# A decoder layer's mixture of experts on one core: chunk of tiles in another order, bias rows and stored residual issued by GpSimd

## The reference, cut to what matters

```python
logits = xt @ w_router + b_router                    # xt: 288 x 1024
top_v, top_i = lax.top_k(logits, 4)
wts = softmax(top_v)
gate_dense = sum(one_hot(top_i, 32) * wts[..., None], axis=1)
out = 0
for e in range(32):                                  # w_up[e]: 1024 x 2048, w_down[e]: 1024 x 1024
    z = xt @ w_up[e] + b_up[e]
    gate = minimum(z[:, :1024], 7.0)
    up = clip(z[:, 1024:], -7.0, 7.0)
    act = (up + 1.0) * gate * sigmoid(1.702 * gate)
    ...                                              # (act @ w_down[e] + b_down[e]), weighted by gate_dense[:, e], is added to out
y = y + g2 * rms_norm(out, norm_ffn_post)            # y: the residual
```

## Time and profile before

| | us |
|---|---|
| median of 3 runs | 1520.52 (1515.4 to 1522.12) |
| the profiled execution's own time | 1513.15 |
| its span, first to last instruction | 1511.3 |
| TensorE busy (matmuls) | 1340.2, 89% of the span |
| TensorE weight loads | 632.4, 42% |
| VectorE, ScalarE, GpSimd busy | 394.7, 254.5, 26.7 |
| moved by DMA | 503.94 MB, mean 333 GB/s |
[...]

### The profile page before, as it was taken

One profiled execution on the slowest core, in us unless ns is written; L12 is line 12 of the kernel. 1 busy time (PEld: TensorE's weight loads), 2 busy tenths in 40 slices (PEclk: granted clock), 3 DMA queues, 4 the chain that ended last, 5 costly groups with the idle time before them and its releaser, 6 DMA issues.

```text
span 1511.3 us, 31712 instructions
## 1 busy us (share of the span) xinstructions
PE 1340.2 (89%) x13949; PEld 632.4 (42%) x13949; DVE 394.7 (26%) x982; ACT 254.5 (17%) x613; POOL 26.7 (2%) x40
## 2 busy tenths in 40 slices
PE   4999997899999897999999789999999669798784
PEld 4554555576765332334333233333343114243231
DVE  5220013378544711112112111221221012021112
ACT  4100006557312200001001000100110001010001
POOL 2000004000000000000000000000000000000000
PEclk9999999999999999999999989999999889999997
DMA  9995746123598799899999996698999999999996
GB/s 282 346 307 217 257 170 196 54 75 139 142 264 333 307 423 426 373 388 393 388 425 427 426 423 290 276 391 355 389 395 424 425 423 428 425 425 425 425 426 235
DMA packets 99297, 503.94 MB, mean 333 GB/s; under 512 B 9473, under 2 KB 39321, under 8 KB 64194
## 3 DMA queue, kind: packets, MB, share of 16 engines
q1 hardware_dynamic: 96258, 485.18, 80.7%
q0 software_dynamic: 2944, 17.32, 3.3%
HBM read 496.33 MB, written 10.31 MB: 335 GB/s over the span
## 4 chain that ended last, share of the span: by engine, by line
PE 65%; DMA 25%; DVE 4%; issue 2%; ACT 1%; POOL 1%; SPq 1%; DVEq 0%; ACTq 0%; POOLq 0%
PE psum L1433 18%; DMA arena<-in_w_down 13%; PE psum L1450 10%; DMA arena<-in_w_up 8%; PE psum L1417 4%; PE psum L819 4%; PE psum L1228 3%; PE psum L1059 3%; PE psum L1060 3%; PE psum L1462 3%; PE psum L1437 2%; PE psum L1325 2%; DMA arena<-in_cache_cmp,arena 2%; PE psum L1468 2%; PE psum L832 1%
## 5 line engine op out<-in xcount | busy, mean ns | idle before, releaser
L1433 PE MATMUL psum<-arena 128*32 128x512 f32 x3328 | 404.5, 621 | 86.0 <-DMA arena<-in_w_up 76.7
L1433 PEld LDWEIGHTS psum<-arena 128*32 128x32 f32 x3328 | 99.5, 112 | 356.3 <-issue 266.0
L1450 PE MATMUL psum<-arena 128*32 128x256 f32 x3328 | 194.1, 383 | 16.3 <-DMA arena<-in_w_down 9.5
L2456 DVE TENSOR_SCALAR arena<-psum 128x256 f32<-128x256 f32 x52 | 22.1, 426 | 662.4 <-PE psum L1433 662.4
L1450 PEld LDWEIGHTS psum<-arena 128*32 128x32 f32 x3328 | 102.4, 110 | 88.2 <-DMA arena<-in_w_down 15.0
L1863 ACT ACTIVATE arena<-arena 128x256 f32<-128x256 f32 x52 | 21.7, 417 | 543.3 <-DVE arena L2456 543.3
L1417 PE MATMUL psum<-arena 128*32 128x256 f32 (+1 forms) x1272 | 94.2, 391 | 3.2 <-DVE arena L2425 3.2
L1228 PE MATMUL psum<-arena 128*128 128x288 f32 x256 | 67.9, 411 | 2.9 <-DMA arena<-in_w_in 2.4
L1417 PEld LDWEIGHTS psum<-arena 128*32 128x32 f32 (+1 forms) x1272 | 30.8, 109 | 83.8 <-issue 78.9
L1462 PE MATMUL psum<-arena 32*128 32x256 f32 x864 | 62.5, 403 | 1.1 <-ACT arena L1872 0.6
L1437 PE MATMUL psum<-arena 32*32 32x512 f32 x416 | 57.8, 627 | 0.0
(11 more groups left out here) (445 smaller groups left out, 1246.3 us busy)
## 6 DMA issues: line engine op xcount, KB each, us to landing
arena<-in_w_up SPq DMA_DIRECT2D x128, 2048.0 KB, 27.5
arena<-in_w_down SPq DMA_DIRECT2D x64, 2048.0 KB, 21.9
arena<-in_w_ada SPq DMA_DIRECT2D x12, 2048.0 KB, 12.4
arena<-in_w_in SPq DMA_DIRECT2D x6, 2048.0 KB, 12.2
arena<-in_w_in SPq DMA_DIRECT2D x16, 512.0 KB, 4.0
arena<-in_state_win SPq DMA_DIRECT2D x4, 1024.0 KB, 10.6
arena<-in_w_out SPq DMA_DIRECT2D x1, 4096.0 KB, 18.4
out<-in_state_win SPq DMA_DIRECT2D x1, 4064.0 KB
```

The costliest lines, as they stand in the source:

```text
L1433: last = mm(banks[0][32 * j:32 * j + SLOT].rearrange("p (h c) -> p h c", h=2), xcT[:, q % 2, q // 2], up_cols[n % R_][:, q % 2, j], start= ...
L1450: last = mm(banks[1][32 * j:32 * j + SLOT, 256:512], aT[:, v, 2 * m + h], down_cols[n % R_][:, h, v, j], start=m + v + h == 0, stop=m + v ...
L2456: V.tensor_scalar(gt, banks[0][:, 0:256], 7.0, None, ALU.min).then_inc(S("gate"), 1)
```

## The change

The ordering within a chunk is changed, and who issues what before the first chunk:
- The b_up matmuls move from after q = 0 to after q = 7, and read row group (r + 2) % 4 for column group r. Directly behind them come the four sample tiles of the dispatch (row group j, column group j) and `add_sample` (row group q, column group (q + 1) % 4). These twelve matmuls use twelve different 32*32 tiles of the array (`small_tiles`). Then come the eight prompt matmuls of the dispatch, `add_prompt`, the transposes of the activations, `chunk_T`, `weights_T`. The last transpose of `weights_T` becomes four 32*32 matmuls with the identity.
- The waits for `oneslot` and `yc` go from behind the up products to behind q = 5. VectorE starts on `up_ps`, signalled by the last b_up matmul.
- To have the sample rows at four partition offsets: ScalarE copies three quarters of h2r's sample rows once, VectorE copies `rowf` and `wts` three times each and completes the one-hot of the first chunk by two operations, all before or at the first chunk.
- GpSimd issues the loads of b_up and b_down, and the two stores of the residual. SyncE's list keeps the pieces; piece 6 waits for `out_ps` alone, piece 8 for the third `h2`, piece 9 for the store. The final sample rows lie rotated by one quarter, with their loads and stores.
- ScalarE takes one square root of a constant into a spare column ahead of the last squares.

```diff
@@ -704,20 +704,11 @@
                     sp.wait_ge(S("out_ps"), 5)
-                    sp.wait_ge(S("h2"), 1)
-                    for r in range(4):
-                        sp.dma_start(bias[32 * r:32 * r + E].rearrange("e (h c) -> e h c", h=2),
-                                     A["b_up"][0].rearrange("e (h j c) -> j e h c", h=2, j=4)[r]).then_inc(S("ld_bias"), 16)
-                    for r in range(4):
-                        sp.dma_start(bdown[32 * r:32 * r + E], A["b_down"][0][:, 256 * r:256 * r + 256]).then_inc(S("ld_bdown"), 16)
                 if n == 8:
-                    sp.wait_ge(S("y1"), 5)
-                    sp.dma_start(xd[0:TP].rearrange("(i p) d -> p i d", p=P), x[:, 0:2]).then_inc(S("st_state"), 16)
-                    sp.dma_start(xd[TP:TP + NS], x[0:NS, 2]).then_inc(S("st_state"), 16)
                     sp.wait_ge(S("h2"), 3)
...
                     sp.wait_ge(S("lg_ps"), 3)
-                    sp.wait_ge(S("st_state"), 64)
+                    sp.wait_ge(S("st_x"), 32)
                 load_piece(n)
@@ -1409,20 +1403,39 @@
 
-            def dispatch(first=False):
-                for n, i in enumerate((0, 2, 1)):
-                    if first and n == 2:
+            def first_dispatch():
+                for n, i in enumerate(ORDER):
+                    if n == 2:
                         pe.wait_ge(S("h2"), 3)
                     for j in range(4):
-                        last = mm(banks[5 if first else 1][32 * j:32 * j + SLOT, 256:512], oneslot[0:ROWS[i], i],
-                                  h2r[0:ROWS[i], i, 256 * j:256 * j + 256],
+                        last = mm(banks[5][32 * j:32 * j + SLOT, 256:512], oneslot[0:ROWS[i], i], h2r[0:ROWS[i], i, 256 * j:256 * j + 256],
                                   start=n == 0, stop=n == 2)
+                last.then_inc(S("xr_ps"), 1)
+
+            def dispatch_prompt():
+                for i in range(2):
+                    for j in range(4):
+                        last = mm(banks[1][32 * j:32 * j + SLOT, 256:512], oneslot[:, i], h2r[:, i, 256 * j:256 * j + 256],
+                                  start=False, stop=i == 1)
                 last.then_inc(S("xr_ps"), 1)
...
                 last.then_inc(S("xcT_ps"), 1)
+
+            def small_tiles(e):
+                if e == 0:
+                    pe.wait_ge(S("ld_bias"), 64)
+                for r in range(4):
+                    at = 32 * ((r + 2) % 4)
+                    last = mm(banks[0][32 * r:32 * r + SLOT, :], ident[at:at + E, at + e:at + e + 1].broadcast_to([E, SLOT]),
+                              bias[at:at + E, :], start=False, stop=True)
+                last.then_inc(S("up_ps"), 1)
+                for j in range(4):
+                    mm(banks[1][32 * j:32 * j + SLOT, 256:512], oneslot[32 * j:32 * j + NS, 2], h2r[32 * j:32 * j + NS, 2, 0:256],
+                       start=True, stop=False)
+                add_sample(owT, yc, SLOT, False, False)
 
@@ -1431,11 +1444,10 @@
                         last = mm(banks[0][32 * j:32 * j + SLOT].rearrange("p (h c) -> p h c", h=2), xcT[:, q % 2, q // 2],
-                                  up_cols[n % R_][:, q % 2, j], start=q == 0, stop=q == 7)
-                    if q == 0:
-                        for r in range(4):
-                            mm(banks[0][32 * r:32 * r + SLOT, :], ident[32 * r:32 * r + E, 32 * r + e:32 * r + e + 1].broadcast_to([E, SLOT]),
-                               bias[32 * r:32 * r + E, :], start=False, stop=False)
+                                  up_cols[n % R_][:, q % 2, j], start=q == 0, stop=False)
+                    if q == 5:
+                        pe.wait_ge(S("oneslot"), c + 2)
+                        pe.wait_ge(S("yc"), c + 1)
                     if q % 2:
@@ -1454,8 +1466,10 @@
                     nc.tensor.transpose(banks[0][:, P * i:P * i + P], ow[:, i].rearrange("p q t -> p (q t)"), ident)
-                nc.tensor.transpose(banks[0][:, TP:TP + NS], ow[0:NS, 2].rearrange("p q t -> p (q t)"), ident[0:NS, 0:NS]
-                                    ).then_inc(S("owT_ps"), 1)
+                for q in range(4):
+                    at = slice(32 * q, 32 * q + NS)
+                    last = mm(banks[0][at, TP:TP + NS], ow[at, 2, q], ident[at, at], start=True, stop=True)
+                last.then_inc(S("owT_ps"), 1)
 
@@ -1465,7 +1479,8 @@
                 for q in range(4):
-                    last = mm(banks[3][32 * q:32 * q + NS, 0:256], shares[32 * q:32 * q + r, TP:TP + NS],
+                    at = 32 * ((q + 1) % 4)
+                    last = mm(banks[3][at:at + NS, 0:256], shares[32 * q:32 * q + r, TP:TP + NS],
                               rows[32 * q:32 * q + r, 0:256], start=start, stop=stop)
@@ -1482,7 +1497,7 @@
             pe.wait_ge(S("oneslot"), 1)
-            dispatch(True)
+            first_dispatch()
             after(pe, "nch")
@@ -1493,7 +1508,7 @@
             add_sample(zeros, zeros, SLOT, True, False)
-            pe.wait_ge(S("ld_bias"), 64)
+            pe.wait_ge(S("h2s"), 3)
 
@@ -1505,18 +1520,16 @@
                     up_products(c, e)
-                    pe.wait_ge(S("oneslot"), c + 2)
-                    pe.wait_ge(S("yc"), c + 1)
-                    dispatch()
+                    small_tiles(e)
+                    dispatch_prompt()
                     for i in range(2):
                         add_prompt(i, owT, yc, SLOT, False, False)
-                    add_sample(owT, yc, SLOT, False, False)
                     pe.wait_ge(S("xr"), c + 2)
-                    chunk_T()
                     pe.wait_ge(S("act"), c + 1)
...
                     last.then_inc(S("aT_ps"), 1)
+                    chunk_T()
                     pe.wait_ge(S("ow"), c + 1)
@@ -1848,6 +1861,9 @@
 
+            act.wait_ge(S("h2"), 1)
+            for j in range(1, 4):
+                nc.scalar.copy(h2r[32 * j:32 * j + NS, 2, 0:256], h2r[0:NS, 2, 256 * j:256 * j + 256]).then_inc(S("h2s"), 1)
             rows_out(0, banks[5])
@@ -1872,6 +1888,7 @@
                 chunk_step(c)
+            fn(rt_[:, 3:4], eps_t, ACT.Sqrt)
             act.wait_ge(S("sums"), 1)
@@ -2415,6 +2432,9 @@
             link(dve, "dve", V.tensor_reduce(rowf[0:NS, 8:12], onr[0:NS, 2], AX, ALU.add))
+            for j in range(1, 4):
+                last = V.tensor_copy(rowf[32 * j:32 * j + NS, 8:12], rowf[0:NS, 8:12])
+            link(dve, "dve", last)
             link(dve, "dve", V.tensor_tensor(in_chunk, rowf.unsqueeze(2).broadcast_to([P, 12, NCHUNK]),
@@ -2434,6 +2454,9 @@
                 link(dve, "dve", V.tensor_scalar(wts[0:r, i], wts[0:r, i], wrec[0:r, i:i + 1], None, ALU.mult))
+            for j in range(1, 4):
+                last = V.tensor_copy(wts[32 * j:32 * j + NS, 2], wts[0:NS, 2])
+            link(dve, "dve", last)
             link(dve, "dve", V.scalar_tensor_tensor(in_chunk, in_chunk, 0.5, wts.rearrange("p i k -> p (i k)").unsqueeze(2).broadcast_to([P, 12, NCHUNK]),
@@ -2445,14 +2468,18 @@
 
+            for at in (slice(32, 64), slice(64, P)):
+                r = at.stop - at.start
+                last = V.tensor_tensor(oneslot[at, 2], C("slot1")[at], slot_of[at, 2, 0:1].broadcast_to([r, SLOT]), ALU.is_equal)
+            link(dve, "dve", last)
             total = dve.value_load(tab[0:1, E - 1:E], min_val=E, max_val=CMAX)
-            dve.wait_ge(S("st_state"), 64)
+            dve.wait_ge(S("st_x"), 32)
             with dve.Fori(0, total) as c:
...
                 one_slot(bass.ds(c + 1, 1))
-                dve.wait_ge(S("up_used"), c * 4 + 4)
+                dve.wait_ge(S("up_ps"), c + 1)
                 V.tensor_scalar(gt, banks[0][:, 0:256], 7.0, None, ALU.min).then_inc(S("gate"), 1)
@@ -2522,6 +2549,16 @@
             gather_selected(7)
+            pool.wait_ge(S("h2"), 1)
+            pool.dma_start(xd[TP:TP + NS], x[0:NS, 2]).then_inc(S("st_x"), 16)
+            for r in range(4):
+                at = 32 * ((r + 2) % 4)
+                pool.dma_start(bias[at:at + E].rearrange("e (h c) -> e h c", h=2),
+                               A["b_up"][0].rearrange("e (h j c) -> j e h c", h=2, j=4)[r]).then_inc(S("ld_bias"), 16)
+            for r in range(4):
+                pool.dma_start(bdown[32 * r:32 * r + E], A["b_down"][0][:, 256 * r:256 * r + 256]).then_inc(S("ld_bdown"), 16)
+            pool.wait_ge(S("y1"), 5)
+            pool.dma_start(xd[0:TP].rearrange("(i p) d -> p i d", p=P), x[:, 0:2]).then_inc(S("st_x"), 16)
 
```

More of the change, by code:

```diff
@@ L730, in _ @@
                     for j in range(4):
-                        sp.dma_start(gate_s[32 * j:32 * j + NS], modd[1:1 + NS, 3 * D + 256 * j:3 * D + 256 * j + 256]
+                        at = 32 * ((j + 1) % 4)
+                        sp.dma_start(gate_s[at:at + NS], modd[1:1 + NS, 3 * D + 256 * j:3 * D + 256 * j + 256]
                                      ).then_inc(S("ld_last"), 16)
@@ L740, in _ @@
             for j in range(4):
```

(8 more changed lines are left out.)

## The result

| | before | after |
|---|---|---|
| median, us | 1521.32 (4 runs, 1515.4 to 1522.65) | 1483.79 (4 runs, 1481.68 to 1484.64) |
| span of the profiled execution, us | 1511.3 | 1482.2 |
| mean granted TensorE clock | 0.971 | 0.953 |

The ratio is 0.976 with a 95% interval of 0.973 to 0.979: 37.5 us less, where 32 from the same median were forecast. The two profiled spans differ by 29.1 us only. Of the 8.4 us between these two figures, 6.2 lie in the part ahead of the experts, whose code the change doesn't touch; it has an experiment of its own (e4). The same comparison, made again later (e8), gave 0.980 (0.977 to 0.983), 29.2 us, so the gain is 29 to 38 us and not a sharp 37.5.

The account below looks back on a forecast made before the run. TensorE bounds stretches with two or more chunks per expert, DMA those with one. Gains of 24 us in the chunks, 6 at the start and 1.3 at the end sum to 31, giving 1489 against 1520.5; range 1477 to 1507.

Parts of the forecast that it names:

- rival 2: Two-chunk stretches: DMA never pauses because the pauses feed themselves; -36 to -44 us, some 1480; chance 0.15.
- The chunk: TensorE's work per chunk: 1.13 us less, 14.92 in place of 16.05, with 0.5 and 1.36 as ends.
- a quarter of the two short groups sticks out: Twelve small tiles in a chunk: overlap not quite full, block 1.09 us between 0.86 and 1.72.
- Rival 1: Small tiles: the three groups don't overlap, 1.72 us, chunk 15.55; -23 us, 1498; chance 0.20.
- The two-chunk stretches: Lost DMA time won back: 8 of 11.9 us from 624 to 835, 8 of 14.9 from 960 to 1158.
- The start: SyncE's queue before the first chunk: bias loads and store moved to GpSimd gain 6 us, ends 0 and 7.5.
- it is done before 520: Residual's store before the first chunk: issued by GpSimd some 3 us earlier on its own queue, finished before 520 us.
- rival 3: Start: store or biases come late through GpSimd and the 6 us are lost; 1495; chance 0.12.
- One-time work: VectorE's additions before chunk 0: 1.3 to 2 us, chunk 0 ends 1 to 2.5 us later, costing nothing.
- The end: After the last chunk: the 1.28 us table load moves to where ScalarE waits for the sums; -1.3 us.
- The base: Whole run: profiled execution 7.4 us below the median of the runs, so 1482 becomes 1489 against 1520.5.
- rival 5: Slower through TensorE's clock; chance 0.04.

Follow-up runs that it names:

- e4: The kernel before, unchanged, traced a second time; 1520.61 us, first piece issued at 471.69 us.
- e8: The kernel after, unchanged, timed again beside the split-store kernel; 1488.45 us, ratio to before 0.980 (0.977 to 0.983).
- e3: The kernel after with b_up, sample dispatch and sample sum all on the same four diagonal tiles; 1500.03 us, ratio to before 0.988.
- e7: The kernel after with one of eight up steps left out of every chunk, all pieces still loaded; 1478.74 us, ratio to before 0.972.
- e2: The kernel before with only the bias loads and the two residual stores moved from SyncE to GpSimd; 1513.99 us against 1517.17, ratio 0.998.
- e6: The kernel after with the residual's 1 MB store cut in two, first half issued earlier; 1481.11 us, ratio to before 0.974; timed again 1482.13, 0.9765.
- e1: The kernel after, but SyncE issues the bias loads and residual stores as before; 1488.3 us, ratio to before 0.981.
- e5: The kernel after without the early square root of a constant; 19.5 us from last landing to end, no whole time given.

## Why the prediction was right, and where its sizes were off

Faster by 32 was forecast from the median shown; 37.5 came, and 29.2 when it was measured again. That is inside the range both times. What happened is faster for the reasons given, between the forecast's own case (31 us) and its rival 2 (36 to 44, DMA never pauses): 37.5 lies in rival 2's figures, 29.2 doesn't, and the table's sum, 35.3, or 33.9 without the clock at the end, lies between. Step by step:

- **Which engine bounds which stretch**: right. e3, after and e7 put three chunk times between 15.5 and 13.8 us on one curve: 15.0 us of time for the first 0.86, 6.8 for the next. An average share of TensorE (87% busy even now) would have promised 52 x 1.42 = 74 us.
- **The chunk**, 1.13 us less forecast, 1.42 came. The term "a quarter of the two short groups sticks out" was wrong by 0.22, 1.21 with its change of tiling against 0.99: overlap is complete. The block behind the transposes was taken as unchanged and gave 0.18, as the activations are transposed first. Against these the other terms of the sum were 0.11 too small, nearly all of it in the dispatch and the prompt sum: 633.65 - 631.57 = 2.08 with their changes of tiling, 1.96 forecast. Rival 1 fell with the trace of the kernel after; e3 shows what it would have looked like. Four b_up matmuls on four row groups write bank 0 within 0.99 us, before and after; each writes other partitions of the bank, and no run has two of them write the same ones.
- **The two-chunk stretches**, 8 + 8 forecast, 10.3 + 12.1 came, and by the forecast's own measure 10.5 + 13.0 of the 26.8 that could be had. This is the term that was mis-sized most, and here rival 2 is nearer than the forecast's own case. Part of it is the shorter chunk: e3 loses 11.4 us more than after in these stretches for 0.86 us a chunk, so 0.28 us (14.92 - 14.64) are some 3.7 us, an estimate on a straight line between the two. The other 2.7 of the 6.4 us were held back for latency after each pause, an estimate that no run isolates; one such case is piece 9 in the kernel after, issued at 529.37 us into a DMA that had run dry, which moved 27 GB/s up to 530.0 and 262 from there to 530.5. The four-chunk expert's 7 is right at 7.1.
- **The start**, 6 forecast, 3.0 came (e2: 3.7). The step that failed is "it is done before 520", 52.5 us behind the first piece; the store landed at 55.6. Pieces 6 and 7 did go 5.5 us earlier, but the store now runs beside the pieces on the DMA engines. The DMA view of the kernel after, by queue: the store's queue (q0) moves nothing up to 515.7 us, 3.9 after the issue; from 515.7 to 521.7 it moves 0.45 MB in 110 packets, 4.1 KB each, while the pieces' queue (q1) moves 1.80 MB in 112, 16.1 KB each; from 521.7 to 523.7 it is 0.54 MB beside 0.26. By then 1.00 of 1.05 MB is through, and the last 0.05 MB, 16 packets, take until 528.5. Piece 9 waited for them, and DMA lost some 3 us. Of rival 3, half came true. e6 takes it back.
- **One-time work**: its price is right, its length not quite. VectorE's additions took 0.51 + 0.51 + 0.39 = 1.4 us. TensorE waited 8.2 us at q = 5 of the first chunk, and the two steps left took 3.28 us in place of 2 x 0.863, at a granted clock of 0.57. The first chunk's down products start 71.2 us behind the first piece in place of 68.0, 3.2 later where 1 to 2.5 were forecast. The landings show no trace of it: piece 27 comes 156.5 us behind the first one in e1 (new chunk order, old queue) and 156.2 and 156.8 in the two traces of before.
- **The end**, 1.3 forecast, 2.7 came, of which 1.4 is the clock of the last down products in this pair of runs (3.33 us at a granted 0.56, and 1.94 at 1.00), not the change. Behind TensorE's last sum it is 12.15 and 10.85 us, the 1.3 of the forecast (e5).
- **The base**: the sum was made against the profiled execution and moved to the median. That execution was a short one: its front part, 467.5 us, is the shortest of eleven. The move was right, and the median before came out at 1517 to 1521 each time. That 1482, the sum without the move, is nearer to 1483.79 than the 1489 forecast is luck: two errors of some 6 us, the short execution and the gain put too low, would have cancelled.
- **The clock** (rival 5): 0.99 to 1.00 in the two-chunk stretches, so they stayed free of what a low clock costs: in the kernel before, eight up records took 1.93 us from 1197.80, at a granted 0.50, and 1.04 from 621.98, at 1.00. The mean fell from 0.971 to 0.953; the low values stand where TensorE waits for pieces, 0.83 from 1171 to 1201 us.

## What to carry to other kernels

Split a run by which bound holds in each stretch and cap every gain by the time that the other resource loses there; here 1.42 us in each of 52 chunks gave 29.6 us and not 74. Small matmuls that can be put on different tiles of the array were had for the time of the longest one, also where they share row and column groups, 0.99 us here against 1.85 on shared ones. A store moved to another queue isn't out of the way (17.5 us to landing, where it was 15.0 on the pieces' queue; cut in two, piece 27 lands 4.4 us earlier, e6): if large transfers run beside it and something waits for it, issue it in parts as early as its data allows.

## What the runs showed of the hardware that I had not expected

Twelve fp32 matmuls on twelve 32*32 tiles, in three groups, took 0.99 us with the change of tiling in the kernel after (630.58 to 631.57), the same as four of them in the kernel before (622.95 to 623.94); on four shared tiles, in e3, 1.85 (628.09 to 629.94). In the kernel after, the second records of the two short groups started at 630.84 and 630.87, those of the b_up group, which stands ahead of them in the program, at 631.03. The store, in packets of 4.1 KB beside the pieces' 16.1, had a fifth of the bytes from 515.7 to 521.7 us (0.45 MB beside 1.80), and its last 0.05 MB took 4.8 us more, from 523.7 to 528.5: 17.5 us from issue to landing for 1 MB. In the kernel before, on the pieces' own queue, it was 15.0: from 509.0 to 519.9 us 16 of 265 packets were under 8 KB, and from 519.9 to 524.5, when those of the two stores ran, 335 of 379.
